# A two-block transformer step on one core: square adds and row loads on GpSimd reordered, four folds moved, gate and up passes interleaved over two PSUM banks

## The reference

```python
def modulate(x, g, c_act, w, b):
    m = c_act @ w + b                                # w is 1024 x 3072, one per sublayer
    shift, scale, gate = jnp.split(m, 3, axis=-1)
    h = rmsnorm(x, g) * (1.0 + scale[:, None, :]) + shift[:, None, :]
    return h, gate[:, None, :]

def swiglu(h, w_gate, w_up, w_down):                 # FF = 2816 = 22 x 128
    return (jax.nn.silu(h @ w_gate) * (h @ w_up)) @ w_down

h, g = modulate(x, norm_g[i, 0], c_act, mod_w[i, 0], mod_b[i, 0])
x = x + 0.5 * g * swiglu(h, ffn_w_gate[i, 0], ffn_w_up[i, 0], ffn_w_down[i, 0])
h, g = modulate(x, norm_g[i, 1], c_act, mod_w[i, 1], mod_b[i, 1])   # then the Mamba-2 mixer
```

## Time and profile before

| | |
|---|---|
| median of 3 runs | 1985.73 us |
| the profiled execution, time | 1991.28 us |
| its span, first to last instruction | 1989.5 us |
| PE busy / DVE / ACT / POOL | 92% / 65% / 47% / 21% of the span |
| share of PE in the chain that ended last | 78% (DVE 11%, ACT 4%, POOL 3%, DMA 1%) |
| mean granted TensorE clock | 0.951 |

### The profile page before, as it was taken

The page is one execution under the profiler, slowest core; times in us unless marked ns, Lnnn a source line. Parts: engine busy times, 40 slices in busy tenths (PEclk is TensorE's granted clock), DMA queues, the critical chain, the costliest instruction groups (busy, mean ns, idle before and its releaser), DMA issues.

```text
span 1989.5 us, 35576 instructions
## 1 busy us (share of the span) xinstructions
PE 1830.8 (92%) x14198; PEld 1753.0 (88%) x14198; DVE 1300.2 (65%) x1797; ACT 942.0 (47%) x1368; POOL 411.5 (21%) x416
## 2 busy tenths in 40 slices
PE   2999899989999999999899998629999999699998
PEld 2999899969999999999699997518999989579998
DVE  6676777888676667768665454994666523566665
ACT  3544455464455554453664543514444311475443
POOL 1222100061222222210321110821222000242221
PEclk9999999999999999999899997868999899699999
DMA  9778634816577556749245542202455334015452
GB/s 377 278 270 295 254 126 171 308 74 253 212 269 282 209 208 260 292 173 358 83 170 190 182 178 105 106 22 106 172 187 190 127 127 148 22 49 185 177 183 84
DMA packets 51058, 371.06 MB, mean 187 GB/s; under 512 B 5665, under 2 KB 5665, under 8 KB 6049
## 3 DMA queue, kind: packets, MB, share of 16 engines
q1 hardware_dynamic: 41760, 302.85, 41.9%
q0 software_dynamic: 9216, 67.11, 8.5%
HBM read 368.89 MB, written 1.05 MB: 186 GB/s over the span
## 4 chain that ended last, share of the span: by engine, by line
PE 78%; DVE 11%; ACT 4%; POOL 3%; issue 2%; DMA 1%; POOLq 0%; SPq 0%; DVEq 0%; ACTq 0%
PE gu L612 14%; PE gu L613 14%; PE gu L614 14%; PE acc L613 7%; PE acc L612 7%; PE acc L614 7%; DVE arena L1972 4%; PE gu L605 3%; PE gu L927 3%; DVE w_lo L1502 2%; PE acc L709 2%; DMA mring<-in_mods 1%; POOL arena L520 1%; DVE arena L1784 1%; PE gu L580 1%
## 5 line engine op out<-in xcount | busy, mean ns | idle before, releaser
L1502 DVE TENSOR_TENSOR w_lo<-ring,w_hi 128x2048 fp32r<-128x2048 f32 x250 | 577.2, 2311 | 274.3 <-ACT w_hi L1181 274.2
L612 PE MATMUL gu<-Hs_hi,w_hi 128*128 128x258 f32 (+1 forms) x2112 | 599.7, 284 | 2.6 <-DVE Hs_lo L1565 2.3
L614 PE MATMUL gu<-Hs_hi,w_lo 128*128 128x258 f32 (+1 forms) x2112 | 599.0, 284 | 0.0
L613 PE MATMUL gu<-Hs_lo,w_hi 128*128 128x258 f32 (+1 forms) x2112 | 598.9, 284 | 0.0
L1181 ACT ACTIVATE w_hi<-ring 128x2048 fp32r<-128x2048 f32 x250 | 476.8, 1908 | 116.6 <-PE acc L614 48.7
L612 PEld LDWEIGHTS gu<-Hs_hi,w_hi 128*128 128x128 f32 x2112 | 403.0, 191 | 4.5 <-issue 1.8
L614 PEld LDWEIGHTS gu<-Hs_hi,w_lo 128*128 128x128 f32 x2112 | 401.4, 190 | 0.0
L613 PEld LDWEIGHTS gu<-Hs_lo,w_hi 128*128 128x128 f32 x2112 | 401.1, 190 | 0.2
L527 POOL TENSOR_TENSOR arena<-arena,rstd 128x512 f32<-128x512 f32 x132 | 193.9, 1469 | 849.1 <-ACT arena L1195 809.7
L613 PE MATMUL acc<-hid_lo,w_hi 128*128 128x256 f32 x1056 | 297.7, 282 | 0.0
L612 PE MATMUL acc<-hid_hi,w_hi 128*128 128x256 f32 x1056 | 295.8, 280 | 1.7 <-DVE hid_lo L1716 1.7
(11 more groups left out here) (296 smaller groups left out, 2726.2 us busy)
## 6 DMA issues: line engine op xcount, KB each, us to landing
ring<-in_weights SPq DMA_DIRECT2D x276, 1024.0 KB, 4.8
mring<-in_mods POOLq DMA_DIRECT2D x64, 1024.0 KB, 6.2
mring<-in_mods SPq DMA_DIRECT2D x8, 1024.0 KB, 7.5
con<-in_constants SPq DMA_DIRECT2D x1, 1408.0 KB, 12.0
X<-in_x SPq DMA_DIRECT2D x1, 1024.0 KB, 7.1
out<-X SPq DMA_DIRECT2D x1, 1024.0 KB, 3.9
cact<-in_c SPq DMA_DIRECT2D x1, 512.0 KB, 3.3
vec<-in_vectors SPq DMA_DIRECT2D x1, 498.0 KB, 4.1
```

Of the source, the lines that this page charges most:

```text
L612: mm(dst, hi, x_hi, start=start, stop=False, skip_group_check=True)
L613: mm(dst, hi, x_lo, start=False, stop=False, skip_group_check=True)
L614: return mm(dst, lo, x_hi, start=False, stop=stop, skip_group_check=True)
L1502: dve.tensor_tensor(w_lo[b][:, :], ring[:, n % RING, :], w_hi[b][:, :].bitcast(F32), ALU.subtract).then_inc(split_ready, 1)
```

## The change

There are three edits.

1. On POOL, the wait for ring slot 1 and the loads of rows 8 to 10 move from ahead of `ffn("ffn0")` to behind the seven square adds of `ffn0`.
2. Rows 20 to 23 are folded at slots 2, 3, 4 and 5 of the last round of `ffn0` instead of 4 to 7, and their successors' loads (rows 23 to 26) move from behind `ffn0` on POOL into it.
3. In all six FFNs the six products of an input tile k are issued in another order: w_hi x_hi for gate and then up, w_hi x_lo for gate and up, w_lo x_hi for gate and up. Before, the three of gate came first and then the three of up. Each half still has its own PSUM bank, so the bank now changes at every matmul instead of at every third.

```diff
+LAST_FOLDS = (2, 3, 4, 5)
...
                     pool.tensor_tensor(sqr[:, 0, :], sqr[:, 0, :], sqr[:, square_at(m), :], ALU.add).then_inc(sq_added, 1)
+                if name == "ffn0":
+                    pool.wait_ge(slot_landed[1], 16)
+                    load_mods(GATE_SLOT, GATE_SLOT + MRING)
                 pool.wait_ge(row_ready, i + 1)
-                folded = [s + 6 * it for it in range(ROUNDS - 1) for s in FOLD_AT] if name in FOLDS else []
+                folded = [s + 2 + 6 * it for it in range(ROUNDS - 1) for s in FOLD_AT] if name in FOLDS else []
+                if name == "ffn0":
+                    folded += [s + 1 + 6 * (ROUNDS - 1) for s in LAST_FOLDS]
...
-                    while done < len(folded) and slot_of(f) >= folded[done] + 2:
+                    while done < len(folded) and slot_of(f) >= folded[done]:
...
-            pool.wait_ge(slot_landed[1], 16)
-            load_mods(GATE_SLOT, GATE_SLOT + MRING)
             ffn("ffn0")
-            load_mods(2 * MSLOTS - 4 + MRING, 2 * MSLOTS + MRING)
...
+            def woven(dsts, w, cols, x_hi, x_lo, start, stop):
+                for i in range(3):
+                    for n, dst in enumerate(dsts):
+                        part = (w_lo if i == 2 else w_hi)[w][:, cols[n]]
+                        ins = mm(dst, part, x_lo if i == 1 else x_hi, start=start and i == 0, stop=stop and i == 2,
+                                 skip_group_check=True)
+                return ins
...
-                        for e in range(2):
-                            ins = three(gu[:, 2 * (f % 2) + e, 0:width], buffer_of(n0, s),
-                                        slice(k * L + e * P, k * L + (e + 1) * P), Hs_hi[:, k, 0:width],
-                                        Hs_lo[:, k, 0:width], start=(k == 0), stop=(k == KD - 1))
+                        ins = woven([gu[:, 2 * (f % 2) + e, 0:width] for e in range(2)], buffer_of(n0, s),
+                                    [slice(k * L + e * P, k * L + (e + 1) * P) for e in range(2)],
+                                    Hs_hi[:, k, 0:width], Hs_lo[:, k, 0:width], start=(k == 0), stop=(k == KD - 1))
...
-                    if n0 == 0 and isinstance(it, int) and it == ROUNDS - 1 and s >= 4:
-                        fold(0, GATE_SLOT + s - 4)
+                    if n0 == 0 and isinstance(it, int) and it == ROUNDS - 1 and s in LAST_FOLDS:
+                        fold(0, GATE_SLOT + LAST_FOLDS.index(s))
```

## The result

The changed kernel takes 1974.87 us (median of 4 runs, 1972.38 to 1976.42); the kernel before took 1986.05 beside it (4 runs, 1985.13 to 1988.01). The ratio is 0.9941, 95% interval 0.9924 to 0.9958: some 11.7 us less, between 8 and 15. The prediction said 1976.8 us, inside 1968 to 1987.

The account below looks back on a forecast made before the run. TensorE was taken to bound the kernel, with time to gain only where it stands still or is slow. Gains of 4.4 (adds), 4.5 (folds) and 0 (interleave), 8.9 us, took the median 1985.73 to 1976.8 us, range 1968 to 1987.

Parts of the forecast that it names:

- What bounds the kernel: Whole kernel: TensorE, on the chain for 78%; time counts only at the head and tail of `ffn0` and in matmul pace.
- Edit 1, the adds: Head of `ffn0`: POOL adds earlier, second pass starts at 43.8 instead of 47.3 us; worth 4.4 us, bounds 3.5 and 5.9.
- The 0.9 for the clock: Behind the second pass's start in `ffn0`: low clock shrinks to 3.4 us, gaining 0.9 us; ends 0 and 2.4.
- The moved loads at no cost: Head of `ffn0`, POOL: issuing the loads later hides beside the wait for the root; cost 0, else 1.78 us.
- ring slots land sooner: Head of `ffn0`: SyncE's ring slots land sooner as the moved row transfers no longer share their DMA engines; no size given.
- Contention of POOL and VectorE: Head of `ffn0`: POOL's adds beside VectorE's `Hs_lo` cost 0, at worst 0.5 us; the last add no longer meets `w_lo`.
- Edit 2, the folds: Tail of `ffn0`: folds off the path, updates of X end at 236.1 instead of 240.7 us; 4.5 us taken.
- its next late wait: Tail of `ffn0`: `w_lo` of Mamba's first slot is late next, behind ScalarE's rounding of that slot, ending at 229.45 us.
- Edit 3, the interleave: Gate-up passes of all six FFNs, 6336 matmuls reordered: pace unchanged, 0 us, bounds -7.8 and +15.5.
- Its own sign of being wrong: Passes at 256 columns: forecast wrong if pace is off 118.9 ns by more than 0.3 ns (2 us).
- the interleave helps: Rival, gate-up passes: pace falls to 117.7 ns, total 1969.0 us; chance 0.16.
- The clock goes down during the passes: Rival, gate-up passes: new order breaks the stream, a tenth of matmuls at low clock, about 2037 us; chance 0.02.

Follow-up runs that it names:

- the four old heads: First gate-up to first down matmul in four kernels that leave the head unchanged (the kernel before among them): 33.5, 32.6, 33.0 and 32.9 us.

## Why the prediction held, step by step

- **What bounds the kernel: right.** All that was gained was gained where TensorE stands still or in its pace. The moved work cost 0.3 us at one place (below) and, as far as the traces show, nothing elsewhere.
- **Edit 1, the adds: right in its path and size.** Predicted were the first add near 35.3, the last end at 41.3 to 41.4, the second pass at 43.8 behind `w_lo`, and 3.4 us of low clock. The trace has 34.97, 41.40, 43.60 and 3.4. The sum was 4.4; against the profiled head of the kernel before the trace gives 4.3, with the edit alone and in all three, and 3.4 to 4.4 against the four old heads. Timed alone it gives 2.6, with an interval up to 4.6, so the size is confirmed in the traces alone. The 0.9 for the clock was taken from one row, and that row is one of two outcomes: the same stop also passed without any low stretch, which was the upper bound.
- **The moved loads at no cost: right, for the reason given.** They hide beside the wait for the root. What I left out is that loads can cost where they stand too early: without their wait they made the kernel 7 us slower. The sentence "ring slots land sooner" was the important one, and it stood there as an aside.
- **Contention of POOL and VectorE: counted 0, it cost 0.3 us.** The last add ran to 41.40 and so did meet `w_lo` of slot 1, which the prediction had ruled out: `w_lo` takes 2.58 us from 40.98, where the one at 224.16 takes 2.29, and the second pass waits for it. That is within the 0.5 named as the worst. The adds themselves took 0.89 us a step. It is POOL's own step and not ScalarE's, whose squares come every 0.71 us and were done at 39.14; 41.40 came out since the four steps of 0.9 that were counted are POOL's. At the tail the contention lies on the chain too: POOL's last scaling begins while a fold runs and takes 2.06 us, where the one at 49.93 takes 1.19 with VectorE idle, and the last SiLU, the rounding and the updates come behind it. It was 2.01 us in the kernel before, so the forecast lost nothing by it, but some 0.9 us may be there for a fold put elsewhere; no run tries it. `hid_lo` takes 1.41 us at 219.38 beside that scaling, and 0.43 at 222.04 with POOL idle; nothing on TensorE waits for the first. The Trainium skill (SBUF — State Buffer, Who interferes with whom) has it that a VectorE instruction with both inputs in SBUF contends with GpSimd's reads; the trace agrees, with these pairs.
- **Edit 2, the folds: right, and its next late wait too.** 4.5 us were forecast; the trace has 4.5 alone and 4.4 with the others, the runs 5.4 (3.6 to 7.2). Row 23 was there in time. The last wait is ScalarE's rounding of Mamba's first slot, as named. The split into 1.3 for the transfer and the rest for two folds is borne out too (1.4 and 3.1).
- **Edit 3, the interleave: the term that was off.** The step that failed is "so the bank does not order them, and I take the row of the same pass: 0". The first half is true where it is tested, at 256 columns; the second doesn't follow: that the bank doesn't set the pace says nothing about the order of the products, which the edit changes as well. From the means, (119.95 - 119.13) x 4224 + (118.95 - 118.69) x 2112 is 4.0 us, less 0.16 x 3168 = 0.5 us that the down passes lose: 3.5, and the runs say 4.4 (2.6 to 6.2). It lay within the bounds (-7.8 to +15.5), and it is the one term that was missing. The step also read its pace from rows of 256 columns alone, while 4224 of the 6336 matmuls have 258. Its own sign of being wrong was a pace off by 0.3 ns at 256 columns; that one moved by 0.26, and the one at 258 by 0.82. The time came out 1.9 us under the forecast. That this is less than 3.5 lies within the spread of the runs and is luck. The rival "the interleave helps" had the right sign and twice the size (7.8).
- **The clock goes down during the passes: wrong, as argued.** The mean granted clock is 0.951 in both. A change of bank at each matmul for six FFNs did nothing to it. The Trainium skill (TensorE: Matmul & The Clock Gate, A second HAM failure mode: psum-queue depth-cycling) puts the case it tells of down to TensorE's short idle times between groups of matmuls; from 49 to 223 us the changed kernel's TensorE waits for nothing, bank changes or not, so its condition isn't met here.

Still open: why the order of products changes the pace by up to 1 ns, and why unchanged down passes move between 117.3 and 118.0 ns when the passes beside them are reordered. The second points away from the operands themselves, but no run here separates it from, say, the place of the instructions in the program. And whether the head is worth 4.3 or 2.6 us.

## What to carry to other kernels

Look at what stands ahead of a critical chain on the queue of a side engine: three DMA issues and the wait that they carried held up the second pass by 3.4 us, and the cure was to put them behind the chain with their wait, since dropping the wait alone made the kernel 7 us slower. Work with no deadline (the folds) goes into the slack of earlier passes, and its loads must move with it; then name the next late wait and take that too. In a stream of thousands of matmuls even the order of equal work is worth a trial: 1 ns is 4 us here at 258 columns; but measure it, for the same order helped one kind of pass, did nothing for another and slowed a third.

## What the runs showed of the hardware

- In the gate-up, down and output-projection passes of these kernels, matmuls of 256 or 258 columns, each with its own weight load, start 117.3 to 120.0 ns apart at full clock, by order and neighbours; at 256 columns the PSUM bank, one or two, made no difference to 0.01 ns.
- The clock's low stretch around a stop of TensorE shrank with the stop: 6.8 us in all four traces where it waited 4.1 us for the adds, and 3.4 us (four traces) or none (three) where it waited 1.5 us for `w_lo`; in one more with this short wait, 6.8 us of low clock lay ahead of it. The same kernel showed both 3.4 and none.
- Where a VectorE and a GpSimd instruction, both with all inputs in SBUF, overlapped, the two took about as long as one after the other: `hid_lo` 1.41 us beside a scaling and 0.43 alone, a scaling 2.06 beside a fold and 1.19 alone, an add 2.60 beside `w_lo` and 0.74 alone.
- Three 1 MB row transfers issued from 28.5 us on instead of 36.4 delayed one 1 MB ring slot from 43.2 to 49.2 us, at a DMA share of 1.01 (1.00 before). It was not the order of issue that decided what landed first: the slot was issued at 27.90 and took 21.3 us, and the row issued at 31.12 took 13.1 and was there 5 us ahead of it.
- Between two executions of one kernel single stretches of low clock come and go, in steps of 1.1 to 1.5 us. Most of the spread between runs of this kernel, some 4 us in four runs, can be such steps.
